# The start-up loads reordered on the two DMA-issuing engines: modulation tiles alone on SyncE, all small rows and both halves of x on ScalarE

## The reference, cut to what matters

```
cond = silu(c)
h = x
for i in range(2):
    mod = cond @ mod_w[i] + mod_b[i]                 # 6 vectors of 1024
    sh1, sc1, g1, sh2, sc2, g2 = split(mod, 6)
    y = rms_norm(h, norm1_g[i]) * (1 + sc1) + sh1
    y = conformer_conv(y) if i == 0 else s5_layer(y)
    h = h + g1 * y
    y = rms_norm(h, norm2_g[i]) * (1 + sc2) + sh2
    y = swiglu(y) if i == 0 else moe_swiglu(y)       # MoE: top 2 of 8 experts
    h = h + g2 * y
out = rms_norm(h, final_norm_g)
```

## Time and profile before

| | |
|---|---|
| median of 3 runs | 1815.11 us (1814.72 to 1815.56) |
| span of the profiled execution, first to last instruction | 1814.6 us |
| PE busy | 1694.3 us, 93% |
| DVE busy | 1392.7 us, 77% |
| ACT busy | 1016.5 us, 56% |
| read from HBM | 461.15 MB, 255 GB/s over the span |

### The profile page before, as it was taken

How to read it: one execution, slowest core, us unless ns; L and a number is a source line. 1 busy time by engine, 2 the same in 40 slices (tenths; PEclk the granted TensorE clock), 3 DMA queues, 4 the chain that set the end, 5 groups by cost and what they waited for, 6 DMA issues and landing times.

```text
span 1814.6 us, 25777 instructions
## 1 busy us (share of the span) xinstructions
PE 1694.3 (93%) x9755; PEld 1428.1 (79%) x9755; DVE 1392.7 (77%) x1405; ACT 1016.5 (56%) x998; POOL 220.3 (12%) x229
## 2 busy tenths in 40 slices
PE   6884899998988979999999999999999999899996
PEld 4663799996443868888888888888888888899996
DVE  4998456667999559889889899898898898544443
ACT  4344545554000447777777687777777876344432
POOL 0342025443655000000000000000000000000000
PEclk8896899998898989999999999999999999899998
DMA  9834267664433369999999999999999999455400
GB/s 303 305 116 158 97 218 253 204 201 170 139 117 115 107 219 352 361 349 363 370 340 361 371 344 359 349 359 371 346 364 367 346 361 364 141 186 175 152 1 35
DMA packets 231198, 463.22 MB, mean 255 GB/s; under 512 B 18255, under 2 KB 57687, under 8 KB 231127
## 3 DMA queue, kind: packets, MB, share of 16 engines
q1 hardware_dynamic: 229591, 461.55, 71.7%
q10 hardware_dynamic: 1536, 0.68, 0.2%
HBM read 461.15 MB, written 1.05 MB: 255 GB/s over the span
## 4 chain that ended last, share of the span: by engine, by line
PE 78%; DVE 16%; ACT 3%; issue 1%; SPq 1%; DMA 0%; ACTq 0%; POOL 0%; DVEq 0%
PE bank L1812 15%; PE bank L1815 15%; PE bank L1818 15%; PE bank L1906 13%; PE bank L1495 11%; PE bank L1642 3%; DVE conv L1099 3%; DVE tmp L1099 2%; DVE xrot L1202 2%; PE bank L1778 1%; DVE xrot L1192 1%; DVE xrot L1196 1%; PE bank L1858 1%; PE bank L1485 1%; ACT yT L643 1%
## 5 line engine op out<-in xcount | busy, mean ns | idle before, releaser
L1370 DVE TENSOR_TENSOR wlo<-ring,whi 128x2048 fp32r<-128x2048 f32 x294 | 667.7, 2288 | 94.9 <-PE bank L1818 76.5
L862 ACT ACTIVATE whi<-ring 128x2048 fp32r<-128x2048 f32 x294 | 561.1, 1918 | 163.5 <-PE bank L1815 163.5
L1812 PE MATMUL bank<-whi,xe_hi 128*128 128x512 f32 x784 | 307.0, 392 | 4.9 <-ACT whi L862 4.9
L1815 PE MATMUL bank<-whi,xe_lo 128*128 128x512 f32 x784 | 306.0, 390 | 0.0
L1818 PE MATMUL bank<-wlo,xe_hi 128*128 128x512 f32 x784 | 209.6, 389 | 0.0
L1425 DVE TENSOR_TENSOR wlo<-ring,whi 128x2048 fp32r<-128x2048 f32 x42 | 96.2, 2293 | 113.9 <-ACT whi L901 86.7
L1812 PEld LDWEIGHTS bank<-whi,xe_hi 128*128 128x128 f32 x784 | 147.7, 188 | 35.8 <-issue 5.1
L1815 PEld LDWEIGHTS bank<-whi,xe_lo 128*128 128x128 f32 x784 | 147.8, 188 | 30.6
L1818 PEld LDWEIGHTS bank<-wlo,xe_hi 128*128 128x128 f32 x784 | 147.3, 188 | 30.7
L1812 PE MATMUL bank<-whi,hh 128*128 128x512 f32 x392 | 157.2, 401 | 0.0
L1815 PE MATMUL bank<-whi,hl 128*128 128x512 f32 x392 | 153.1, 391 | 0.0
(11 more groups left out here) (339 smaller groups left out, 2742.3 us busy)
## 6 DMA issues: line engine op xcount, KB each, us to landing
ring<-in_moe_w_gate_dram SPq DMA_DIRECT2D x112, 1024.0 KB, 7.0
ring<-in_moe_w_up_dram SPq DMA_DIRECT2D x112, 1024.0 KB, 7.1
ring<-in_moe_w_down_dram SPq DMA_DIRECT2D x112, 1024.0 KB, 6.7
ring<-in_mod_w_dram SPq DMA_DIRECT2D x24, 2048.0 KB, 9.0
ring<-in_ffn_w_gate_dram SPq DMA_DIRECT2D x11, 1024.0 KB, 6.4
ring<-in_ffn_w_up_dram SPq DMA_DIRECT2D x11, 1024.0 KB, 9.1
ring<-in_ffn_w_down_dram SPq DMA_DIRECT2D x11, 1024.0 KB, 5.1
ring<-in_conv_w_pw_dram SPq DMA_DIRECT2D x8, 1024.0 KB, 10.9
```

The lines of the kernel that those rows point to most:

```text
L862: act.activation(whi[:, n % HI_SLOTS, :], ring[:, s * HW:(s + 1) * HW], ACT.Copy).then_inc(hi_ready, 1)
L1370: v.tensor_tensor(wlo[:, n % LO_SLOTS, :], ring[:, s * HW:(s + 1) * HW], whi[:, n % HI_SLOTS, :].bitcast(F32), ALU.subtract).then_inc(lo_r ...
L1812: mm(o[:, :], xh, hi[:, w:w + 512], start=first, stop=False)
L1815: ins = mm(o[:, :], xl, hi[:, w:w + 512], start=False, stop=False)
```

## The change: what it does

SP no longer issues the first half of x or any row: its program begins with the four modulation tiles. ACT issues the conditioning row, then both halves of x, then the other 15 rows. Nothing else differs; the waits and semaphores are the same.

```diff
         @block.sync
         def _(sp):
 
-            sp.dma_start(x_tok[:, 0, :], x[0, 0:P, :]).then_inc(x_in, 16)
-            load_rows(sp, ROW_NAMES[1::2])
             for n, (kind, i) in enumerate(STREAM):
...
         @block.scalar
         def _(act):
-            load_rows(act, ROW_NAMES[0::2])
-            act.dma_start(x_tok[:, 1, :], x[0, P:2 * P, :]).then_inc(x_in, 16)
+            load_rows(act, ROW_NAMES[:1])
+            for tb in range(TB):
+                act.dma_start(x_tok[:, tb, :], x[0, tb * P:(tb + 1) * P, :]).then_inc(x_in, 16)
+            load_rows(act, ROW_NAMES[1:])
```

## The result

The changed kernel took 1820.43 us (median of 6 runs, 1819.79 to 1820.84) against 1814.91 us (6 runs, 1814.46 to 1815.56): a ratio of 1.0026, 95% interval 1.0016 to 1.0036. It is slower by 5.5 us, where 0.4 us faster was forecast. Measured once more, beside other runs of both, the difference was 3.9 us (1819.81 against 1815.91 us, ratio 1.0021, 1.0012 to 1.0030).

What follows compares the result with a forecast made beforehand. Before 51 us DMA was taken as the bound, setting when DVE's convolution starts. Earlier tiles -1.5 us and late rows +1.1 made -0.4: span 1814.6 to 1814.2, plus 0.5 for the median, 1814.7 us; range 1812.3 to 1820.0.

Steps and rivals of the forecast that it cites:

- Part 1: SP's start-up issues go: first modulation tile issued 3.67 us earlier, fourth in 1.48 us earlier, at about 29.3.
- Part 2: ACT issues 18 DMAs instead of nine: log_dt issued at about 8.0 in place of 3.99 us.
- way A: DMA path to the convolution start (L1085): pw1's issue, S5 loads, DVE's S5 blocks; expected to decide, at 50.7 us.
- part 3: Small rows share DMA engines with the modulation stream: x runs 2.9 to 7.0 us, rows complete at 13.2.
- d: Delay of the rows' completion at start-up against the kernel before: 5.6 us forecast, lower bound 4.0.
- R3: Rival: longer DMA queue turns, each ACT DMA waiting for 8 pieces; rows at about 16.8, +3.2 us, 1818.3; chance 0.13.
- part 5: pw1's bytes start at 30.4 us, craw lands 13.0 later at 43.4, convolution starts at 50.7: -0.4 us.
- R2: Rival: SP's held start-up issues also hold ACT's, delaying the rows; 1820.0 or 1825 us; chance 0.13.
- R1: Rival: S5 loads behind pw1 go out sooner, up to 4.9 us less (1810.2), likelier 1812.5; chance 0.08.
- R4: Rival: TensorE's clock falls, so PE's path decides the convolution start; +0.8 us, 1815.9; chance 0.18.
- way B: PE path to the convolution start: modulation, yT, products with pw1, sigmoid; forecast done at 46.2 us, not deciding.
- Part 4: Serial chain from rows to first modulation product passes the rows' delay whole: pw1 issued at 28.4, not 22.83 us.

Runs made afterwards that it cites:

- rows ahead of x: The changed kernel with ACT issuing all 16 rows first and both halves of x last; 1816.75 against 1815.72 us (ratio 1.0006).
- before, x ahead: The kernel before with ACT issuing x's second half right behind c, ahead of its other rows; 1815.77 against 1816.88 us (ratio 0.9997).
- x early, rows shared: The changed kernel with x right behind c on ACT and the rows shared between SP and ACT; 1815.10 against 1815.91 us (ratio 0.9996).
- held for c: The changed kernel with SP waiting until c has landed before issuing the first modulation tile; 1818.33 us (ratio 1.0014).
- half of x on SP: The changed kernel with x's first half issued by SP ahead of the modulation tiles; 1818.00 against 1815.72 us (ratio 1.0009).
- held for x: The changed kernel with SP waiting for both halves of x before issuing the first modulation tile; 1818.87 us in one run.
- one tile ahead: The changed kernel with SP issuing one modulation tile, then waiting for both halves of x before the second; 1818.04 us in one run.

## Why the prediction was wrong

Part 1 was right and a little small: the fourth modulation tile landed 2.1 us earlier (1.5 forecast), and PE's wait for it was gone. Part 2 was right: the issue of log_dt at 8.26 (8.0). The order of the steps was right too: way A decides, with nothing for the time won on the tiles.

**The step that failed is part 3, where x was put to start at 2.9 us, "some 1.5 us after their issue".** It started at 5.4, 4.0 us after its issue. From there the sum held: x took 4.1 us (4.1 forecast), the rows 5.7 us (5.5), the count 0.8 (0.7). Those 2.5 us are nearly the whole distance between the d of 5.6 us forecast and the 8.3 us measured. The row that could have told it was there: in the earlier trace rows the first modulation tile, issued 0.15 us behind x, had only 3 packets on the way 2.3 us later. I read it as longer turns (R3), and in part 5 as 2.0 us from any issue to its first byte; that the tile was the later of two issues was left out. With nothing ahead of them the first tile moved 1.1 us after its issue in the changed kernel, and pw1 1.0 us after. The one-to-one of the earlier trace rows was right, and says nothing of the first wait. R3 gave d = 9.2, nearer than the forecast, but by a cause that fell: the turns were one to one. (Its upper bound is mis-added too: 17 pieces for each of 18 DMAs make a d of 23, not 21.) R2 fell as well: ACT's issues were not held. Its price of 1820.0 is nearest to the 1820.43 measured, by luck. R1 fell: the tail got longer, not shorter. And R4 had the clock right and not its effect: the granted clock fell to 0.50 from 44 to 46 us, way B ended at 51.90 (51.43 + 0.47) where part 6 had 46.2, and it still had 3.9 us to spare.

Two terms more were too small. From the rows to pw1's issue the distance grew by 1.0 us (9.3 against 8.3), all of it in the sum of squares, 6.72 us against 5.70. Part 4 took it for fixed. In the twelve profiles it takes 3.72 to 6.72 us, and kernels that are alike up to this sum scatter as much as the term itself: 5.70 and 6.36 without the change, 6.72, 5.43 and 5.25 with it. So this 1.0 us can't be put down to the change; the 3.72 of the kernel with the rows ahead of x lies outside that scatter, and its cause is open. TensorE at one or the other of its levels would do this (this line's products take 379 ns at the shortest and 797 at the longest), but the granted clock reads 1.00 throughout, so this stays an inference. And in part 5 the distance from the issue of pw1 to craw was 16.3 us, not 15.0. Its two terms were 1.0 and 15.3, and not 2.0 and 13.0. The 13.0 was counted in the kernel before from 30.8, as if pw1 began when the last modulation tile had landed. But there it was on its way before that. The queue from 28.8 to 30.8 us:

```profile
q1 hardware_dynamic: 662, 0.70, 105.2%
```

662 packets for 0.70 MB can't be pieces of 2 KB; with pw1's of 1 KB among them they make some 0.65 MB of pw1, an estimate, or 1.9 us at that rate. In the changed kernel nothing of pw1 overlaps with the last tile.

The sum closes: 2.7 for the rows, 1.0 for the sum of squares, 1.3 for the tail make 5.0; L1085 was forecast at 50.7 and began at 55.77.

The kernels together show the hinge of part 5, pw1's issue against L1085 (without the two in which the S5 loads go ahead of pw1; with the rows ahead of x the last to come is x, at 16.48):

| kernel | rows complete | pw1 issued | L1085 |
|---|---|---|---|
| before | 7.64 | 22.83 | 51.08 |
| before, x ahead | 8.94 | 24.88 | 50.55 |
| rows ahead of x | 12.31 | 26.83 | 51.04 |
| x early, rows shared | 11.11 | 27.02 | 50.80 |
| held for c | 13.51 | 28.73 | 52.54 |
| half of x on SP | 14.06 | 28.88 | 52.60 |
| held for x | 13.62 | 29.00 | 52.92 |
| one tile ahead | 14.32 | 30.46 | 54.24 |
| changed, again | 15.99 | 30.91 | 54.76 |
| changed | 15.96 | 32.17 | 55.77 |

Up to an issue at 26.8 us the start of the convolution hardly depends on it; from 27.0 on it follows at a distance of 23.6 to 23.9 us. The prediction had the hinge at 27.3 (d = 4.5), which was right, and a distance of 22.3, which was 1.4 short. What part 1 was to gain shows at most as 0.5 us, in the second row.

Behind L1085 the shift was still 4.5 us at 582 us, and 3.5 us from 604 us on. Between them lie TensorE's products of the S5 layer, in which the granted clock fell and rose at other points (from 582 to 588 us it was 0.54 before and 1.00 after), so the last 1 us is put down to the clock and not to the change, which no run tests; in the repeated profile it was 3.7 at L1085 and 4.3 at the end. The difference of one pair of profiles is therefore good to about 1 us, and the medians, 5.5 and 3.9 us apart in two measurements, enclose the 4.7 of L1085.

## What to carry to other kernels

Ask of a start-up load not only how many bytes stand ahead of it but when the first answer is needed: here 240 KB of small rows gate the request for the next 2 MB, and to put them behind a stream that nobody awaits before 20 us emptied the DMA engines for over 4 us later on. When two engines issue, it was the order in time of the issues that counted in these runs, across both queues, so issue the small and urgent transfers before any deep one, on whichever engine. If one engine must issue both large and small, the small go first: with that order the changed kernel was 1.0 us slower than the kernel before and not 5.5, though in its profile part of this came from a shorter sum of squares, whose cause is open.

## What the runs showed of the hardware

A transfer issued on ACT's queue behind the first tile on SP's did not move for 2.3 to 4.4 us, while 7 to 34 pieces an engine went by, with one tile ahead of it or with more. The other way round, SP's stream, issued at 2.33 behind x, had no packet before 5.5. Only from then on did the queues take turns, 33 packets to 37, then 72 to 79, in half a microsecond. The Trainium skill ("DMA: Bandwidth & Descriptors", section "Queues, rings and completion order") has the engines switch queues after a packet of typically 9 to 17 descriptors. If a piece here is a descriptor, which these runs do not show, the first wait was from 7 to 34 of them, so no such count explains it, and the turns afterwards look like single pieces in the sums over 16 engines. What the waiting transfer waits for, and where it is held, these runs do not show.

A held issue of SP did not hold ACT's: SP's four issues took 13.35 us, the third of them 6.22 from 1.91 on, while ACT issued 18 transfers at 0.31 to 0.61 us each.
